# Router logits with their weights held in TensorE, a mean over a pre-added pair of chunks, and an earlier pair of gating rows in a two-layer hybrid trunk

## What is computed

```
proj = h @ w_in ;  a, b, p, gc, gp = split(proj)
u    = a * sigmoid(b)                                  # 512 channels
u    = causal depthwise conv of u, 31 taps, + bias
u    = silu(layer_norm(u))                             # mean and variance over the 512 channels
yc   = u @ w_conv_out
yp   = (window means of p minus p) @ w_pool * pool_scale
x    = x + (sigmoid(gc) * yc + sigmoid(gp) * yp) @ w_out
layer 0:  x = x + dense SwiGLU(rms_norm(x))
layer 1:  logits = rms_norm(x) @ router_w              # 1024 x 8
          x = x + sum over the top 2 of 8 experts of share * SwiGLU_e(rms_norm(x))
out  = rms_norm(x) * final_norm
```

## Time and profile before

| | |
|---|---|
| runs, median | 1428.15 us (1425.51 to 1428.62) |
| the profiled execution, its own time | 1425.18 us |
| its span in the trace | 1423.6 us |
| PE busy | 1409.4 us, 99% |
| weight loads busy | 1168.6 us, 82% |
| DVE busy | 1174.7 us, 83% |
| ACT busy | 986.9 us, 69% |
| POOL busy | 207.9 us, 15% |
| DMA | 445.96 MB, mean 313 GB/s |

### The profile page before, as it was taken

The page is one execution under the profiler, slowest core; times in us unless marked ns, Lnnn a source line. Parts: engine busy times, 40 slices in busy tenths (PEclk is TensorE's granted clock), DMA queues, the critical chain, the costliest instruction groups (busy, mean ns, idle before and its releaser), DMA issues.

```text
span 1423.6 us, 18360 instructions
## 1 busy us (share of the span) xinstructions
PE 1409.4 (99%) x6506; PEld 1168.6 (82%) x6506; DVE 1174.7 (83%) x1068; ACT 986.9 (69%) x876; POOL 207.9 (15%) x249
## 2 busy tenths in 40 slices
PE   9999999999999999999999999999999999999997
PEld 7888888888888888888888888888888888888885
DVE  6987544548987998889899898888989989888896
ACT  7765444347765877867877777786787777778674
POOL 6840000005831001001001001000100100100010
PEclk9999999999999999999999999999999999999999
DMA  9656555545548899999999999999999999999990
GB/s 359 222 169 215 178 181 198 183 162 196 175 164 310 283 386 378 371 370 409 375 382 372 390 367 371 388 370 369 412 372 384 370 391 366 371 389 373 366 411 33
DMA packets 197552, 445.96 MB, mean 313 GB/s; under 512 B 8400, under 2 KB 19968, under 8 KB 197504
## 3 DMA queue, kind: packets, MB, share of 16 engines
q1 hardware_dynamic: 192496, 432.57, 80.4%
q0 software_dynamic: 2304, 8.39, 2.2%
q10 hardware_dynamic: 2704, 4.38, 0.9%
HBM read 437.97 MB, written 7.34 MB: 313 GB/s over the span
## 4 chain that ended last, share of the span: by engine, by line
issue 58%; PE 34%; POOL 4%; DVE 2%; ACT 1%; DMA 0%; POOLq 0%; ACTq 0%; DVEq 0%
PE bank L1467 10%; PE bank L1469 10%; PE bank L1468 10%; POOL small L611 2%; POOL gates L614 2%; DVE w_lo L989 1%; POOL sums L621 1%; PE bank L1528 1%; DVE bank L1038 1%; PE bank L1631 0%; PE bank L1593 0%; ACT w_hi L654 0%; PE bank L1763 0%; PE bank L1587 0%; DVE tokA L1104 0%
## 5 line engine op out<-in xcount | busy, mean ns | idle before, releaser
L989 DVE TENSOR_TENSOR w_lo<-raw,w_hi 128x2048 fp32r<-128x2048 f32 x256 | 582.9, 2292 | 134.8 <-ACT w_hi L654 134.6
L654 ACT ACTIVATE w_hi<-raw 128x2048 fp32r<-128x2048 f32 x256 | 488.6, 1913 | 200.2 <-PE bank L1469 199.8
L1467 PE MATMUL bank<-w_hi,dT_hi 128*128 128x512 f32 (+1 forms) x756 | 296.4, 392 | 0.0
L1469 PE MATMUL bank<-w_hi,dT_lo 128*128 128x512 f32 (+1 forms) x756 | 293.2, 388 | 0.0
L1468 PE MATMUL bank<-w_lo,dT_hi 128*128 128x512 f32 (+1 forms) x756 | 292.6, 387 | 0.0
L1467 PE MATMUL bank<-w_hi,cT_hi 128*128 128x512 f32 x492 | 194.3, 395 | 0.0
L1469 PE MATMUL bank<-w_hi,cT_lo 128*128 128x512 f32 x492 | 191.7, 390 | 0.0
L1468 PE MATMUL bank<-w_lo,cT_hi 128*128 128x512 f32 x492 | 191.6, 390 | 0.0
L1469 PEld LDWEIGHTS bank<-w_hi,dT_lo 128*128 128x128 f32 x756 | 142.0, 188 | 29.4
L1467 PE MATMUL bank<-w_hi,hT_hi 128*128 128x512 f32 x416 | 164.4, 395 | 1.1 <-DVE w_lo L1086 1.0
L1468 PEld LDWEIGHTS bank<-w_lo,dT_hi 128*128 128x128 f32 x756 | 142.2, 188 | 28.1
(11 more groups left out here) (256 smaller groups left out, 1865.8 us busy)
## 6 DMA issues: line engine op xcount, KB each, us to landing
raw<-in_moe_w_gate_dram SPq DMA_DIRECT2D x96, 1024.0 KB, 7.5
raw<-in_moe_w_up_dram SPq DMA_DIRECT2D x72, 1024.0 KB, 10.3
raw<-in_moe_w_down_dram SPq DMA_DIRECT2D x72, 1024.0 KB, 8.9
raw<-in_w_in_dram SPq DMA_DIRECT2D x20, 1024.0 KB, 7.1
mix<-in_moe_w_up_dram SPq DMA_DIRECT2D x16, 1024.0 KB, 8.8
gates<-in_moe_w_down_dram SPq DMA_DIRECT2D x16, 1024.0 KB, 11.3
gates<-in_moe_w_up_dram SPq DMA_DIRECT2D x16, 1024.0 KB, 8.8
work<-in_moe_w_down_dram SPq DMA_DIRECT2D x16, 1024.0 KB, 11.5
```

Source lines behind the costliest of these rows:

```text
L654: act.activation(w_hi[split_place(u, seen.item is not None)][:, 0:width], place[slot][:, 0:width], ACT.Copy).then_inc(hi_ready, 1)
L989: dve.tensor_tensor(w_lo[split][:, 0:width], place[slot][:, 0:width], w_hi[split][:, 0:width].bitcast(F32), ALU.subtract).then_inc(lo_read ...
L1467: nc.tensor.matmul(dst, a_hi, b_hi, start=start, stop=False)
L1469: return nc.tensor.matmul(dst, a_lo, b_hi, start=False, stop=stop)
```

## The change

Three things change.

1. `u_rows(1, ...)` of both mixers is issued before three convolution taps instead of behind them.
2. The mean: POOL adds chunks 0 and 1 into a free buffer of the product ring (`two_chunks`) after its last product, and PE runs three matmuls instead of four, the first of them waiting for that sum.
3. The router: the 16 columns of router weights, with what stands behind them (a zeroed block), become the stationary operand and 256 turned tokens stream past, high part and rest, in 16 matmuls instead of 32. The result has the logits in 16 rows; ACT copies them to `logits_T`, and PE turns them and adds high and rest in two small matmuls against `fold`, an 8 x 8 identity stacked twice. DVE then copies the logits once instead of copying and adding. ACT's high part of token block 0 becomes DVE's, to leave ACT free for that copy, and the ranks come two products later.

```diff
+        two_chunks = tap_prod[:, PRODS - 1, :]
+        rw_wide = spreadT[:, :, :].rearrange("p b t -> p (b t)")
-        LOGITS, RANK, TOTAL = R_HIGH, 3, R_HIGH[1]
+        LOGITS_T, LOGITS, RANK, TOTAL = R_HIGH[0], R_HIGH[1], 3, R_HIGH[1]
...
 POOL, router constants
+                pool.tensor_tensor(fold[0:2 * E, :], ident[0:2 * E, 0:E], ident[0:2 * E, E:2 * E], ALU.add)
 POOL, behind the adds of a mixer
+                pool.wait_ge(prod_added, len(ADDS) * (l + 1))
+                pool.wait_ge(conv_step, CONV_STEPS * l + TAPS + 1)
+                pool.tensor_tensor(two_chunks, conv[:, 0, :], conv[:, 1, :], ALU.add).then_inc(chunks_added, 1)
 ACT, router
-            for b in range(TB):
-                act.activation(xn_hi[b], xs[:, b, :], ACT.Copy, scale=rstd(b)).then_inc(xn_hi_ready, 1)
+            act.activation(xn_hi[1], xs[:, 1, :], ACT.Copy, scale=rstd(1)).then_inc(xn_hi_ready, 1)
+            act.wait_ge(logits_done, 1)
+            act.activation(logits_T[0:2 * E, :], bank[LOGITS_T][0:2 * E, 0:S], ACT.Copy).then_inc(logits_copied, 1)
 DVE, mixer
                 split_to(U + 6)
+                u_rows(1, M.high)
                 conv_taps(13)
-                u_rows(1, M.high)
 DVE, router
+            dve.tensor_scalar(spreadT[:, 1, :], ident[:, :], 0.0, None, ALU.mult).then_inc(pad_ready, 1)
...
+            step(dve.tensor_scalar(xn_hi[0], xs[:, 0, :], rstd(0), None, ALU.mult))
             xn_rest(0)
...
-            dve.wait_ge(logits_done, seen.next(logits_done))
-            for b in range(TB):
-                ins = dve.tensor_copy(route[:, T2, b, :], bank[LOGITS[b]][:, 0:E])
-            step(ins)
-            for b in range(TB):
-                ins = dve.tensor_tensor(LG[:, b, :], bank[LOGITS[b]][:, E:2 * E], route[:, T2, b, :], ALU.add)
-            step(ins)
+            dve.wait_ge(logits_turned, 1)
+            step(dve.tensor_copy(LG, bank[LOGITS][:, 0:TB * E].rearrange("p (b e) -> p b e", b=TB)))
 PE, statistics
-                    for c in range(CC):
...
-                        last = nc.tensor.matmul(bank[M.mean][:, 0:S], mean_w[:, :], conv[:, c, :], start=c == 0, stop=c == CC - 1)
+                    pe.wait_ge(chunks_added, l + 1)
+                    nc.tensor.matmul(bank[M.mean][:, 0:S], mean_w[:, :], two_chunks, start=True, stop=False)
+                    for c in (2, 3):
+                        pe.wait_ge(conv_step, CONV_STEPS * l + {2: CONV_STEPS - 1, 3: CONV_STEPS}[c])
+                        last = nc.tensor.matmul(bank[M.mean][:, 0:S], mean_w[:, :], conv[:, c, :], start=False, stop=c == CC - 1)
 PE, router
             def logits(k):
-                for b in range(TB):
-                    for part in (hT_hi, hT_lo):
-                        last = nc.tensor.matmul(bank[LOGITS[b]][:, 0:2 * E], part[:, k, b * P:(b + 1) * P],
-                                                rw_parts[:, k, :], start=k == 0 and part is hT_hi,
-                                                stop=k == KD - 1 and part is hT_lo)
+                for part in (hT_hi, hT_lo):
+                    last = nc.tensor.matmul(bank[LOGITS_T][:, 0:S], rw_wide[:, 2 * E * k:2 * E * k + P], part[:, k, :],
+                                            start=k == 0 and part is hT_hi, stop=k == KD - 1 and part is hT_lo)
                 return last
+            def turn_logits():
+                pe.wait_ge(consts_ready, 3)
+                pe.wait_ge(logits_copied, 1)
+                for b in range(TB):
+                    last = nc.tensor.matmul(bank[LOGITS][:, E * b:E * (b + 1)], logits_T[0:2 * E, b * P:(b + 1) * P],
+                                            fold[0:2 * E, :], start=True, stop=True)
+                last.then_inc(logits_turned, 1)
...
-                            if (j, b, kk) == (1, 1, 0):
+                            if (j, b, kk) == (1, 0, 0):
+                                turn_logits()
+                            if (j, b, kk) == (1, 1, 1):
                                 ranks()
```

More of the change, by code:

```diff
@@ L298, in trunk_kernel @@
         pair = carve(8, TB)
+        logits_T = carve(S)
+        fold = carve(E)
+        assert carved[0] <= (PRODS - 1) * S
+        two_chunks = tap_prod[:, PRODS - 1, :]
         token = sb("token", [P, TB, 4], F32R)
@@ L357, in trunk_kernel @@
         uT_done, uT_ready, conv_step = sem("uT_done"), sem("uT_ready"), sem("conv_step")
-        prod_ready, prod_added = sem("prod_ready"), sem("prod_added")
+        prod_ready, prod_added, chunks_added = sem("prod_ready"), sem("prod_added"), sem("chunks_added")
         pooled_done, dT_hi_ready, dT_ready = sem("pooled_done"), sem("dT_hi_ready"), sem("dT_ready")
@@ L371, in trunk_kernel @@
         logits_done, diff_ready, probs_ready = sem("logits_done"), sem("diff_ready"), sem("probs_ready")
+        logits_copied, logits_turned, pad_ready = sem("logits_copied"), sem("logits_turned"), sem("pad_ready")
         mask_ready, rank_done, total_done, tables_ready = sem("mask_ready"), sem("rank_done"), sem("total_done"), sem("tables_ready")
@@ L1242, in xn_rest @@
             def xn_rest(b):
-                dve.wait_ge(xn_hi_ready, b + 1)
                 return dve.scalar_tensor_tensor(xn_lo[b], xs[:, b, :], rstd(b), xn_hi[b].bitcast(F32), ALU.mult, ALU.subtract)
             dve.wait_ge(rstd_ready, seen.next(rstd_ready))
+            step(dve.tensor_scalar(xn_hi[0], xs[:, 0, :], rstd(0), None, ALU.mult))
             xn_rest(0)
@@ L1277, in _ @@
             dve.tensor_scalar(token[:, :, 1], row_no[:, :], 0.0, 1.0, ALU.mult, ALU.add)
+            dve.wait_ge(xn_hi_ready, 1)
             xn_rest(1)
@@ L1581, in statistics @@
                 def statistics():
-                    for c in range(CC):
-                        if c == 1:
-                            pe.wait_ge(prod_added, len(ADDS) * l + last_add[c])
-                        else:
-                            pe.wait_ge(conv_step, CONV_STEPS * l + {0: TAPS + 1, 2: CONV_STEPS - 1, 3: CONV_STEPS}[c])
-                        last = nc.tensor.matmul(bank[M.mean][:, 0:S], mean_w[:, :], conv[:, c, :], start=c == 0, stop=c == CC - 1)
+                    pe.wait_ge(chunks_added, l + 1)
[3 more added lines that the diff above has]
+                        last = nc.tensor.matmul(bank[M.mean][:, 0:S], mean_w[:, :], conv[:, c, :], start=False, stop=c == CC - 1)
                     last.then_inc(mean_done, 1)
@@ L1709, in logits @@
             def logits(k):
-                for b in range(TB):
-                    for part in (hT_hi, hT_lo):
-                        last = nc.tensor.matmul(bank[LOGITS[b]][:, 0:2 * E], part[:, k, b * P:(b + 1) * P],
-                                                rw_parts[:, k, :], start=k == 0 and part is hT_hi,
-                                                stop=k == KD - 1 and part is hT_lo)
-                return last
+                for part in (hT_hi, hT_lo):
+                    last = nc.tensor.matmul(bank[LOGITS_T][:, 0:S], rw_wide[:, 2 * E * k:2 * E * k + P], part[:, k, :],
+                                            start=k == 0 and part is hT_hi, stop=k == KD - 1 and part is hT_lo)
+                return last
+            def turn_logits():
+                pe.wait_ge(consts_ready, 3)
+                pe.wait_ge(logits_copied, 1)
+                for b in range(TB):
+                    last = nc.tensor.matmul(bank[LOGITS][:, E * b:E * (b + 1)], logits_T[0:2 * E, b * P:(b + 1) * P],
+                                            fold[0:2 * E, :], start=True, stop=True)
+                last.then_inc(logits_turned, 1)
             def ranks():
@@ L1749, in gate_of_all_tokens @@
                             pe.wait_ge(rw_ready, 1)
+                            pe.wait_ge(pad_ready, 1)
                     if j == 0:
```

## The result

The changed kernel took 1430.93 us (median of 14 runs, 1429.35 to 1431.89), the kernel before 1427.27 us (median of 14 runs of its own on the same chip, 1425.22 to 1429.83). The ratio is 1.0028, with an interval of 1.0021 to 1.0036: 3.7 us more, where 1.95 us more was forecast (the range reached 1432.0 us). The profiled execution took 1430.28 us with a span of 1428.6 us, 5.1 us more than the profiled execution before. The medians are the measure; the traces tell where it goes.

What follows compares the result with a forecast made beforehand. PE, busy 99% of the span, was taken as the bound; +2.15 us from mixers (already swallowing the u rows' 1.60) and -0.2 from the router made +1.95, so 1428.15 became 1430.1 us, range 1427.8 to 1432.0.

Steps and rivals of the forecast that it cites:

- Rows of u: Second turn of u: rows come about 1.2 us earlier, PE wins 1.03 us in layer 0 and 0.57 in layer 1.
- the sum: Whole kernel: +2.15 us for the mixers and -0.2 us for the router, +1.95 us in all.
- The mean: First mean matmul waits for POOL's new add: +1.05 us in layer 0, +1.10 us in layer 1.
- The rival in which POOL's end follows PE: Mixers: POOL's end follows PE or its add is seen quicker, +0.7 us or less there, about 1428.6 us; chance 0.18.
- The router up to the gather: Logits to gather: logits matmuls save 1.81 us, PE alone wins 1.3, and is 1.15 us ahead after a 0.15 wait.
- covered: Ranks: the mask stands at about 455.3 us and PE reaches the ranks at 455.7, so no wait.
- just covered: One-hot matrix: ready at about 457.8 us, PE needs it at 457.9.
- the 455.7 of the working: Ranks: the time in us at which PE reaches them, given as two product triples less the gain later.
- does not move: First expert slab: rests of the gathered tokens keep their start, slack 0.25 us, so the router gives only -0.2 us.
- the rival in which POOL and DVE exclude each other: Router: POOL's 2.87 us first, PE waits 2.0 to 2.5 at the ranks, about +3.5 in all; 0.17 with clock rival.
- A fall at the mean: PE's clock falls in the wait before the mean, costing 2 us or more, 1432 us or more; 0.17 with exclusion rival.

Runs made afterwards that it cites:

- e1: Kernel before with only the second pair of u rows moved ahead of three taps: 1425.06 us, ratio 0.9997.
- e2: Kernel before with only POOL's sum of chunks 0 and 1 and three mean matmuls: 1429.74 us, ratio 1.0024.
- e7: Changed kernel with the mean as before and one tap of chunk 3 moved from ACT and POOL to DVE: 1427.37 us, ratio 1.0006.
- e3: Kernel before with only the router part of the change: 1427.47 us, ratio 1.0006.
- e5: Changed kernel with ACT's two stores of x issued behind the high parts of the gathered tokens: 1427.97 us, ratio 1.001.
- e6: Changed kernel with eight unused 512-column matmuls between the gather and the first expert slab: 1430.22 us, ratio 1.0023.
- e10: Changed kernel with the four mean matmuls put back and POOL's extra add taken out: 1427.02 us, ratio 1.0012.
- e4: Changed kernel with ACT making both xn_hi blocks again and DVE making the rest of block 1 first: 1428.76 us, ratio 1.0015.
- e9: Kernel before with the pre-added mean and three more unread matmuls in PE's wait for POOL's sum: 1429.41 us, ratio 1.002.
- e8: Changed kernel with four mean matmuls, one tap moved to DVE, ACT making both xn_hi blocks, and later stores of x: 1424.42 us, ratio 0.9985.

## Why the prediction was right in its direction and too small

**Rows of u: right.** PE won 1.00 and 0.57 us at the two turns (in layer 1 it stands 0.93 us late ahead of the turn and 0.36 behind the wait), against 1.03 and 0.57. The two means swallowed it, as the sum assumed; without the pre-add 0.54 of it would have stayed (e1).

**The mean: right, in mechanism and size.** Forecast +1.05 and +1.10, measured +0.90 and +1.12; waits of 2.30 and 2.07 us against 2.5 and 2.1. The stretch from the first mean load to the first pooling load is 1.19 us, not 1.30. A figure beside the sum is too high: the earlier trace rows give 2.45 less 0.74, 1.7 us for a split, not 1.9. The rival in which POOL's end follows PE did not come. What the table cannot tell, e2 and e7 do: the pre-add costs 2.25 us alone, and a POOL with one product fewer lets PE keep nearly everything.

**The router up to the gather: half the size.** From the first logits matmul (449.03) to the product behind the last one (453.12) PE needs 4.09 us instead of 5.77: it won 1.68 us, against 1.81 forecast. But 1.15 us were to be left at the gather, and 0.52 were. The turn was late by about 0.3 us instead of 0.15, the ranks by 0.35 (forecast covered) and the one-hot matrix by 0.2 (just covered). The mask came at 458.10 us, 456.05 without the mixers' shift, as late as in before and 0.75 later than forecast, since one small DVE instruction of the selection (L1276) took 0.88 us instead of 0.18. It begins 0.26 us behind the start of POOL's second instruction, here and in e3, e5, e6, e7 and e10, and takes 0.87 or 0.88 us in each; why is open. The ranks stand one product triple later in PE's order, not two; the 455.7 of the working is already the time for one.

**The first expert slab: this is the step that failed.** The prediction said that what PE needs next "does not move", with a slack of 0.25 us, and so the router gives -0.2 us. It did move, by 1.37 us more than the mixers' shift (3.42 less 2.05 on ACT). Measured: -0.52 + 1.83 = +1.31 us, and e3 has +1.3 alone. Two things had been left out. The first was POOL's stretch of 0.55 us beside DVE's new high part. I had it as a rival, but priced it as POOL holding DVE back by a full 2.87 us. It went the other way: both began together, DVE's instruction was done in 0.75 us, and POOL paid. The ranks, which that rival made late by 2.0 to 2.5 us, were late by 0.35. The Trainium skill, "SBUF — State Buffer", section "Who interferes with whom", counts a `tensor_scalar` in a two-port mode among the instructions that exclude GpSimd; here the trace agrees with it in so far as POOL is stretched (3.42 instead of 2.87 us), by less than the 0.75 us of that instruction. The `scalar_tensor_tensor` of the same size beside the same POOL instruction gives no single answer: it cost nothing in before and e4 (1.28 and 1.29 us), and took 1.94 us here. The second was a length, not a start. I took the time that ACT's two stores of x need, 1.92 us, as fixed, and they took 2.74. Taking DVE's instruction away saves 1 us (e4), moving the stores removes the whole wait (e5). The longer issue is no accident of one execution: it takes 1.92 or 1.93 us in before, e1, e2 and e9, which have the old router, 2.70 to 2.85 in the changed kernel, e3, e6, e7 and e10, and 2.30 in e4. What in the new router lengthens it is open.

**The clock.** A fall at the mean was a rival, since that wait is the longest. There, at 2.30 us, the clock stayed at 1.00. It fell after the wait of 1.87 us at the first expert slab, which at 1.84 us in e3 and 1.97 in e10 was followed by none. Its cost was not in the sum. How often it comes can only be guessed from the mean clock of an execution, which is rounded and also takes in the end of the program, where several traces have a fall too. It is 0.997 or less in 14 of 14 executions of the changed kernel and in 12 of 35 of before on the chip of e1. At 1.6 us for two thirds more of the executions this gives about 1 us, an estimate that no run checks. The 14 executions of before in the comparison itself fall into two groups, seven from 1425.2 to 1426.7 us and seven from 1427.8 to 1429.8. Their median lies between, and the changed kernel has no lower group. So the medians differ by 3.66 us and the two profiled executions, the one of before from the lower end, by 5.10.

**The sum again.** +2.02 - 0.52 + 1.83 = +3.33 us from the stages, and about 1 us for the clock if the estimate holds, against 3.66 between the medians. In the profiled executions the same steps with 1.44 for the fall and 0.4 behind it make 5.2. The parts measured alone give -0.4, +3.4 and +0.9 by their ratios, 3.9 together. The measured change is near the 3.5 us of the rival in which POOL and DVE exclude each other; that is luck, since the wait of 2.0 to 2.5 us at the ranks on which that number stood did not come. It is luck too that 1430.93 us lies only 0.8 us from the forecast 1430.1: the forecast started from the median of three executions of before, 0.9 us above the median of fourteen.

**Open.** What decides on a fall of the clock at 452 to 470 us. It came with PE idle ahead of it (after, e7) and with PE busy (e1, e2, e9); by the mean clock (0.997 or less) it came in ten or all of eleven executions of e2, e9 and e7, but in two of ten of e8. The pre-add is not needed for it (e7), though the changed kernel with it has 14 of 14 and without it five of eleven (e10), and the idle time at the mean is not its cause (e9). Nor is it simply how late PE arrives: e4 has the mixers of the changed kernel, and six of its eleven executions are at 0.998 or more. No run here separates the arrival from the transfers around it.

## What to carry to other kernels

An instruction saved on the bounding engine is worth nothing where its operand comes last, and less than nothing where saving it adds a link behind that operand: read the slack of each operand before counting instructions. When work moves to another engine, price what it does to the instructions that run beside it and to the queue behind them, even where it fits an idle gap. And when a result says that a path "does not move", check the durations on it as well as their starts.

## What the runs showed of the hardware

- A `tensor_scalar` of 128 x 1024 from float32 to fp32r on DVE took 0.75 us, and POOL's instruction that began with it 3.42 instead of 2.87; the DVE instruction behind it took 1.94 instead of 1.28. Six kernels show the same three durations within 0.01 us. With ACT making the same rows (e4, e8), POOL and DVE kept their old durations.
- A `TENSOR_TENSOR` of 16 columns on DVE that began 0.26 us behind the start of a POOL `tensor_scalar` of 128 x 1024 took 0.87 or 0.88 us in those six kernels, instead of 0.18.
- The clock went to 1.2 GHz with PE recorded busy in every stretch ahead of it (e1, e2, e9), and stayed at 2.4 GHz across a wait of 2.30 us. After a wait for the same operand it fell at 1.84 and 1.87 us (e7, the changed kernel) and did not at 1.84 and 1.97 (e3, e10). A fall lasted about 3.4 us and cost 1.4 to 1.6 us.
- The same two DMA issues on ACT took 1.92 us in the kernel before, 2.30 in e4 and 2.74 in the changed one, each time directly behind two others, and 0.78 us together when issued over 5 us behind those (e5, e8). With them out of the way the chain behind began 2.4 us sooner.
